# Moving the first output tile's products into the last attention head, and joining two score matmuls of the even stage

## The chip, the cores and the metric

One core of a Trainium2 chip runs the whole program once. The metric is the device time of that core in microseconds (us). TensorE (PE) does matmuls and transposes, with a separate record for each weight load (PEld); VectorE (DVE), ScalarE (ACT) and GpSimd (POOL) do the rest; SyncE (SP) issues most transfers. Each engine works through its own queue in order, and semaphores tie the queues together.

## The reference, cut to what matters

Two layers on 1024 latent and 256 context tokens of width 1024. Layer 0 is an "even" mixer: input projections, a short convolution, an mLSTM over ten chunks of 128 tokens in two directions for four heads of width 256, and an output projection. Layer 1 is latent attention with 16 heads, and again an output projection over 2048 rows, followed by a layer norm:

```
# mlstm, per chunk                       # attention, per head
s   = einsum('bhtd,bhsd->bhts', qc, kc) * w     s = einsum(q_n, k_n) + einsum(q_r, k_r)
num = einsum('bhts,bhsd->bhtd', s, vc) + ...    p = softmax(s * MLA_SCALE)
kw  = kc * w_tok                                o = einsum('bhqk,bkhd->bqhd', p, v)
# after all heads
y_lat = (o_lat * silu(s_lat[3])) @ w_out        # 1024 x 2048 @ 2048 x 1024
h_lat = layer_norm(DEEPNORM_ALPHA * h_lat + g_l * y_lat, ...)
```

## The kernel before, in words

Every float32 product is made of three matmuls on operands split into a high and a low part in the type fp32r: `mm3` (lines 37 to 42) issues high x high, high x low and low x high into one accumulation. ACT makes the high part by a cast, DVE the low part by a subtraction. One weight load goes with each matmul.

**Even stage** (`stage_even`). PE walks through 18 projection tiles a head, and other work is put between them. `prepare(h, c)` (from line 1069) is such work: for a chunk `c` it makes the 128 x 128 scores of keys and queries, two `mm3` (one for each half of the head's width, so six matmuls of 128 columns), and two transposes of the keys, all into one PSUM bank. `prepared(h, c)` (line 913) is DVE's side: it copies the scores to `v_s_all` (line 917) and the turned keys to `v_k_tok` (line 918), and frees the bank. `PREPARED` (line 403) puts the ten chunks two by two at five places of tiles 4 and 5, for four heads. The chunks of such a pair go to two different banks (`e_e` and `e_z` in the rows).

**Attention** (`stage_attend`). A slot is a head `h` and a tile `t` of 128 queries, eight to a head, 128 in all. In a slot PE makes the scores (line 2389: five matmuls for each of 256, 512 and 512 keys) in the three-bank tensor `S`; DVE finds the maximum in two parts and the bias (lines 2281 to 2285); ACT takes the exponential (line 2193); DVE inverts the total (line 2289) and ACT normalises (line 2198). PE's next scores wait for that exponential, since it reads `S` (line 2399). In between PE turns the probabilities of the slot before by ten transposes (`T` operations, line 2376), whose results ACT and DVE split into `t_pt_hi` and `t_pt_lo`. Twice a head PE multiplies them with the values (`PV`, line 2383, 30 matmuls of 512 columns), at `t` = 5 and at `t` = 1 of the next head. In the other slots PE projects queries, keys and values of the next head. The last head, 15, has no next head, so its slots hold no projections. `T`, `PV` and projections write a ring of five PSUM banks in turn, and an operation waits until the one five earlier is read (`RING`, line 2368).

**Output stage** (`stage_out`, layer 1). A token tile's result is 16 steps `k`, each with two halves `o`: six matmuls of 512 columns for one tile and `k`. `first_pair` (line 1479) does tiles 0 and 1 together, `k` by `k`, as weight `k` becomes ready (`w_ok`), with the last three `T` operations before `k` = 1 and the last `PV` before `k` = 2; then tiles 2 to 7 follow one by one. Before it PE waits for the last exponential (`scores_read`) and for the low part of `T(15, 6, 2)` (`ring_read`), whose bank tile 1 takes. Weights are split by ACT (line 1235) and DVE (line 1244): w0, w1 and the first halves of the inputs of tiles 0 and 1 (`m`) in slots 1 and 5 of the last head (`OUT_SPLITS`), w2 to w5 behind the last `T` operations (`OUT_TAIL`), the others in `stage_out` (`REST`). SP loads w8 to w11 after the last scores, w12 after the last `T`, and the second halves of `m` and w13 to w15 after the last `PV`.

Of the kernel before, what the change touches and what calls it, by code (L numbers as in the profile page):

```python
# [6 lines left out]
D = 1024  # L7
CTX, LAT = 256, 1024
T = CTX + LAT
P = 128  # L10
# [5 lines left out]
KM = MIX // P  # L16
# [367 lines left out]
def stage_even(nc, a, keep):  # L384
# [49 lines left out]
    with ExitStack() as ctx:  # L434
# [364 lines left out]
        def _(dve):  # L799
# [239 lines left out]
        def _(pe):  # L1039
# [29 lines left out]
            def prepare(h, c):  # L1069

                t0, bank = c * P, prep_bank(c)
                pe.wait_ge(pj_free_d, dve_free[(h, 3, group_of(c))])
                if c >= 2:
                    pe.wait_ge(prep_ok, prep_at[(h, c - 2)])
                elif h:
                    pe.wait_ge(ht_used, ht_at[(h - 1, 1, 2)])
                else:
                    pe.wait_ge(const_ok, 1)
                    pe.wait_ge(g_kept, 10)
                for j in range(2):  # L1080
                    mm3(nc, bank[:, 0:P], (k_hi[:, j, t0:t0 + P], k_lo[:, j, t0:t0 + P]), (q_hi[:, j, t0:t0 + P], q_lo[:, j, t0:t0 + P]), j == 0, j == 1)
                for j in range(2):
                    last = nc.tensor.transpose(bank[:, (1 + j) * P:(2 + j) * P], k_whole[:, j, t0:t0 + P], ident[:, :])
                last.then_inc(prep_done, 1)

            def state(h, n, d):
# [94 lines left out]
class Output:  # L1181
# [46 lines left out]
    def high(self, act, kind, n, h=None):  # L1228
# [4 lines left out]
        else:  # L1233
            act.wait_ge(self.w_in[n % OUT_HALF], 16 * (n // OUT_HALF + 1))
            self.nc.scalar.copy(self.w_hi[n][:, :], self.w_raw[n][:, :]).then_inc(self.w_hi_ok, 1)

    def low(self, dve, kind, n, h=None):
        if kind == "m":
            b = self.slot(n, h)
            dve.wait_ge(self.m_hi_ok, self.order_of[(n, h)])  # L1240
            self.nc.vector.tensor_tensor(self.m_lo[b][:, :, :], self.m_raw[b][:, :, :], f(self.m_hi[b][:, :, :]), ALU.subtract).then_inc(self.m_ok, 1)
        else:
            dve.wait_ge(self.w_hi_ok, n + 1)
            self.nc.vector.tensor_tensor(self.w_lo[n][:, :], self.w_raw[n][:, :], f(self.w_hi[n][:, :]), ALU.subtract).then_inc(self.w_ok, 1)


def stage_out(nc, a, keep, layer, out=None, block=None, latent=None, tail=None):
# [10 lines left out]
    with ExitStack() as ctx:  # L1258
# [212 lines left out]

        @block.tensor
        def _(pe):
            def products(n, k, o):
                b, i = slot(n, k // H), k % H
                return mm3(nc, y_bank[n % YB][o], (m_hi[b][:, i, :], m_lo[b][:, i, :]), (w_hi[k][:, cols(o)], w_lo[k][:, cols(o)]),
                           k == 0, k == KM - 1)

            def first_pair():

                for k in range(KM):
                    if layer == 1:
                        for op in tail["ring_ops"].get(k, ()):
                            tail["ring_op"](op)
                    pe.wait_ge(w_ok, k + 1)
                    for n in range(2):
                        if k % H == 0:
                            pe.wait_ge(m_ok, order_of[(n, k // H)])
                        for o in range(2):
# [3 lines left out]
                    if k == H - 1:  # L1493
                        last.then_inc(first_half, 1)

            def project(n, between=()):
# [447 lines left out]
def stage_attend(nc, a, keep):  # L1944
# [48 lines left out]
    with ExitStack() as ctx:  # L1993
# [6 lines left out]
        def pair(name, shape, where, step):  # L2000
# [29 lines left out]
        ROW, lq_at, lkv_at = 8 * D, keep["t_at"]["lq"], keep["t_at"]["lkv"]  # L2030
        v_at, prob_at, turn_at = u_at + 16 * T + 24 * LAT, u_at + 32 * T + 24 * LAT, u_at + 40 * T + 24 * LAT
        places = {"w": [lkv_at, lkv_at + 16 * T, lkv_at + 16 * T + ROW, lat_at, lq_at, lq_at + ROW, lq_at + 2 * ROW, lat_at + ROW,
                        u_at + 8 * T, u_at + 16 * T + 8 * LAT, u_at + 16 * T + 16 * LAT, lkv_at + 8 * T, prob_at, v_at, v_at + ROW, w_at],
                  "m": [u_at, u_at + 16 * T, w_at + ROW, pt_at], "res0": pt_at + ROW, "res1": pt_at + ROW + 4 * D, "y0": pt_at + 2 * ROW,
                  "y1": v_at + 2 * ROW, "g_bc": turn_at, "ln_g": w_at + 2 * ROW, "ln_b": w_at + 2 * ROW + 4 * D, "small": turn_at + 4 * LAT}
        last, end = AH - 1, ("PV", AH - 1, 1)
        old, third = ("T", last, QT - 2, 2), [("T", last, QT - 1, g) for g in range(2)]
        y_banks = [[S[:, 0:512], S[:, 512:1024]], [S[:, 1024:1536], ring[at[old] % RING][:, :]], [ring[at[op] % RING][:, :] for op in third]]
# [5 lines left out]
        bank = lambda op: ring[at[op] % RING]  # L2044
        tile = lambda h, t: h * QT + t

        LOADS, load_no = hw.order, hw.load_no
# [13 lines left out]
        def place(op, half):  # L2061
# [6 lines left out]
            if kind == "v":  # L2068
# [5 lines left out]
        tail = {"ring_ops": {1: TAIL[:3], 2: TAIL[3:]}, "scores_read": (exp_ok, tile(last, QT)), "ring_read": (ring_free, at[old]),  # L2074
                "third_banks": (ring_free, at[third[1]]), "values_done": (ring_done, at[end]),
                "queries_split": (qs_ok, AH + 1), "stored": [(og_out[x], 16 * AH) for x in range(2)]}

# [1 line left out]
        def _(sp):  # L2079
# [41 lines left out]
            sp.wait_ge(ring_done, at[("T", last, QT - 1, 2)])  # L2121
            out.load_w(sp, 12)
            store(last, 1)
            sp.wait_ge(ring_done, at[end])
            sp.wait_ge(og_out[0], 16 * AH)
            out.load_m(sp, 0, 1)
            out.load_m(sp, 1, 1)
            for k in range(13, KM):
                out.load_w(sp, k)
            sp.wait_ge(og_out[1], 16 * AH)  # L2130

# [26 lines left out]
        def _(act):  # L2158
# [45 lines left out]
            for h, t in slots:  # L2204
                turned = turned_ops(moved(h, t))
                if not values(h, t):
                    for op in turned[:1]:
                        high(op)
                    exponentials(h, t)
                    for op in turned[1:]:  # L2210
                        high(op)
                    normalise(h, t)
                else:
                    exponentials(h, t)
                    normalise(h, t)
# [12 lines left out]
                if split_here(h, t) and not values(h, t):  # L2228
                    split(*split_here(h, t))
            for op in TAIL:  # L2230
                high(op)
            for piece in OUT_TAIL:
# [3 lines left out]
        def _(dve):  # L2236
# [58 lines left out]
            for h, t in slots:  # L2295
                turned = turned_ops(moved(h, t))
                maximum(h, t)
                earlier = (h, t - 1) if t else (h - 1, QT - 1)
                if split_here(*earlier) and not values(*earlier):
                    hw.low(dve, *split_here(*earlier))  # L2300
# [27 lines left out]
        def _(pe):  # L2328
# [36 lines left out]

            def ring_op(op):
                n, ps = at[op], bank(op)
                if n > RING:
                    pe.wait_ge(ring_free, n - RING)
                if op[0] == "T":  # L2370
                    _, h, t, g = op
                    if g == 0:
# [11 lines left out]
                else:  # L2384
                    weights_ok(op)
                    last = project(op, ps)
                last.then_inc(ring_done, 1)

            def scores(h, t):
                b, tok = h % 2, slice(t * P, (t + 1) * P)  # L2390
# [124 lines left out]
```

## Time and profile before

| | us |
|---|---|
| median of 3 runs (lowest, highest) | 2916.73 (2914.29, 2917.38) |
| the profiled execution's own time | 2915.16 |
| its span, first to last instruction | 2913.4 |
| PE busy | 2861.9 (98%) |
| DVE busy | 1534.6 (53%) |
| ACT busy | 1192.5 (41%) |

A row of the timeline gives the start in us from the span's start, the duration, the engine, line, operation, output and inputs, and in brackets how long the engine was idle before it and what released it. A matmul's duration includes its way through the array, so that the records of neighbouring matmuls overlap; what a matmul costs in a row of matmuls is the distance from its start to the next start.

### The profile page before, as it was taken

Reading aid. Unit: us, or ns where it says so; the run is one execution under the profiler, and the core shown is the slowest. Engines: PE = TensorE matmul, PEld = TensorE weight load, DVE = VectorE, ACT = ScalarE, POOL = GpSimd, SP = SyncE. Lnnn points to the kernel's source line nnn. Section 1 sums busy time; section 2 is a strip of 40 time slices with the busy share of each in tenths; the row PEclk is TensorE's granted clock in tenths of the full one; section 3 lists DMA queues with packets and bytes.
Section 4 is the critical chain, followed back from the end, with each engine's and each line's share of the span. In section 5 each row is a group of like instructions: output and inputs, shape, how many; then the busy total and the mean of one; then the engine's idle time right before and its main releaser. Section 6 shows DMA issues by size and latency. Waiting matters only on the chain. (4 is left out here: it accounts for less than half of the span.)

```text
span 2913.4 us, 38355 instructions
## 1 busy us (share of the span) xinstructions
PE 2861.9 (98%) x15527; PEld 2455.1 (84%) x15527; DVE 1534.6 (53%) x2782; ACT 1192.5 (41%) x1991; POOL 261.1 (9%) x279
## 2 busy tenths in 40 slices
PE   7999999999999999999999999999999999999998
PEld 6888888888888888888887887888888888888787
DVE  6646543655256536554353324665656666666544
ACT  6323312332233223342244214666666666666500
POOL 5100000000000000001320001202102022020000
PEclk9999999999999999999999999999999999999999
DMA  7311131123111311163361320100000101002332
GB/s 210 96 33 46 46 112 31 46 55 112 31 46 46 114 30 46 53 212 102 109 194 42 116 94 26 34 27 30 27 26 27 38 19 34 23 27 98 123 94 79
DMA packets 221505, 200.77 MB, mean 69 GB/s; under 512 B 12085, under 2 KB 193221, under 8 KB 221330
## 3 DMA queue, kind: packets, MB, share of 16 engines
q1 hardware_dynamic: 208578, 184.91, 20.7%
q0 software_dynamic: 2352, 8.17, 0.8%
q10 hardware_dynamic: 10400, 5.24, 0.6%
q8 instruction: 124, 2.03, 0.3%
q14 instruction: 51, 0.42, 0.0%
HBM read 157.34 MB, written 40.95 MB: 68 GB/s over the span
## 5 line engine op out<-in xcount | busy, mean ns | idle before, releaser
L40 PE MATMUL e_pj<-e_u_hi,v_w_hi 128*128 128x512 f32 (+1 forms) x864 | 310.1, 359 | 1.9 <-DVE v_kk_lo L878 1.9
L40 PE MATMUL e_pj<-e_u_hi,e_w_hi 128*128 128x512 f32 (+1 forms) x864 | 308.1, 357 | 1.0 <-PEq L58 1.0
L41 PE MATMUL e_pj<-e_u_lo,v_w_hi 128*128 128x512 f32 (+1 forms) x864 | 308.3, 357 | 0.0
L42 PE MATMUL e_pj<-e_u_hi,v_w_lo 128*128 128x512 f32 (+1 forms) x864 | 308.1, 357 | 0.0
L41 PE MATMUL e_pj<-e_u_lo,e_w_hi 128*128 128x512 f32 (+1 forms) x864 | 306.0, 354 | 0.0
L42 PE MATMUL e_pj<-e_u_hi,e_w_lo 128*128 128x512 f32 (+1 forms) x864 | 305.8, 354 | 0.0
L2177 ACT CAST t_pt_hi<-t_ring 128x512 fp32r<-128x512 f32 (+1 forms) x384 | 181.6, 520 | 233.0 <-PE t_ring L2376 233.0
L2264 DVE TENSOR_TENSOR t_pt_lo<-t_ring,t_pt_hi 128x512 fp32r<-128x512 f32 (+1 forms) x384 | 216.2, 598 | 52.0 <-ACT t_pt_hi L2177 50.7
L2193 ACT ACTIVATE t_prob<-t_scores,t_bias 128x1280 f32<-128x1280 f32 x128 | 170.7, 1334 | 90.9 <-DVE t_bias L2285 90.6
L40 PEld LDWEIGHTS e_pj<-e_u_hi,v_w_hi 128*128 128x128 f32 x864 | 164.9, 191 | 24.5 <-DVE v_kk_lo L878 2.1
L42 PEld LDWEIGHTS e_pj<-e_u_hi,v_w_lo 128*128 128x128 f32 x864 | 164.6, 190 | 23.7
L41 PEld LDWEIGHTS e_pj<-e_u_lo,v_w_hi 128*128 128x128 f32 x864 | 164.8, 191 | 21.4
L42 PEld LDWEIGHTS e_pj<-e_u_hi,e_w_lo 128*128 128x128 f32 x864 | 163.1, 189 | 23.2
L40 PEld LDWEIGHTS e_pj<-e_u_hi,e_w_hi 128*128 128x128 f32 x864 | 163.2, 189 | 22.1 <-issue 1.2
L41 PEld LDWEIGHTS e_pj<-e_u_lo,e_w_hi 128*128 128x128 f32 x864 | 163.3, 189 | 20.6
L2198 ACT ACTIVATE t_prob<-t_prob,t_rec 128x1280 f32<-128x1280 f32 x128 | 177.2, 1384 | 7.4 <-DVE t_rec L2289 7.4
L2376 PEld LDWEIGHTS t_ring<-k_ident,t_prob 128*128 128x128 f32 x1280 | 147.2, 140 | 16.7
L2376 PE MATMUL t_ring<-k_ident,t_prob 128*128 128x128 f32 x1280 | 160.3, 272 | 0.0
L40 PE MATMUL t_scores<-t_kn_hi,t_qn_hi 128*128 128x512 f32 (+1 forms) x384 | 141.5, 369 | 9.0 <-ACT t_prob L2193 7.5
L41 PE MATMUL t_scores<-t_kn_lo,t_qn_hi 128*128 128x512 f32 (+1 forms) x384 | 136.7, 356 | 0.0
L2405 PE MATMUL t_scores<-l_kr_lo,t_qs 128*128 128x512 f32 (+1 forms) x384 | 136.6, 356 | 0.0
L2404 PE MATMUL t_scores<-l_kr_hi,t_qs 128*128 128x512 f32 (+1 forms) x384 | 136.5, 355 | 0.0
(461 smaller groups left out, 6650.7 us busy)
## 6 DMA issues: line engine op xcount, KB each, us to landing
e_w_raw<-in_ev_w_in SPq DMA_DIRECT2D x72, 512.0 KB, 4.7
v_mw<-in_mod_w SPq DMA_DIRECT2D x32, 512.0 KB, 4.0
l_w_raw<-in_od_w_in SPq DMA_DIRECT2D x21, 512.0 KB, 4.0
o_m_raw<-mixT SPq DMA_DIRECT2D x20, 512.0 KB, 5.4
o_w_raw<-in_ev_w_out SPq DMA_DIRECT2D x16, 512.0 KB, 10.4
zgT<-l_lat_q SPq DMA_DIRECT2D x16, 512.0 KB, 3.8
t_zg<-zgT SPq DMA_DIRECT2D x32, 256.0 KB, 2.8
ogT<-t_zg SPq DMA_DIRECT2D x32, 256.0 KB, 2.0
```

The lines of the kernel that those rows point to most:

```text
L40: nc.tensor.matmul(out, whi, xhi, start=first, stop=False)
L41: nc.tensor.matmul(out, whi, xlo, start=False, stop=False)
L42: return nc.tensor.matmul(out, wlo, xhi, start=False, stop=last)
L2177: nc.scalar.copy(dst, src).then_inc(ring_hi, 1)
L2193: nc.scalar.activation(prob[x][:, :], S[:, 0:T], ACT.Exp, bias=bias[x][:, :], accum_out=total[x][:, :]).then_inc(exp_ok, 1)
L2198: nc.scalar.mul(prob[x][:, :], prob[x][:, :], rec[x][:, :]).then_inc(prob_ok, 1)
L2264: nc.vector.tensor_tensor(dst, src, hi, ALU.subtract).then_inc(ring_free, frees(op))
L2376: last = nc.tensor.transpose(ps[:, c * P:(c + 1) * P], prob[t % 2][:, (c0 + c) * P:(c0 + c + 1) * P], ident[:, :])
L2404: nc.tensor.matmul(out, qs[b][:, tok], kr2[0][:, k0:k0 + n], start=False, stop=False)
L2405: last = nc.tensor.matmul(out, qs[b][:, tok], kr2[1][:, k0:k0 + n], start=False, stop=True)
```

## The change: what it does

In the even stage the high and low queries lie in one tensor `q_both`, and one matmul of 256 columns multiplies the high keys with both; a second one, of 128 columns, multiplies the low keys with the high queries. That makes four matmuls for a chunk where there were six. The bank then holds two partial score blocks side by side, and DVE adds them with a `tensor_reduce` over pairs where it copied.

In attention, six steps of output tile 0 (`k` = 0 to 5) are done in slots 2 to 7 of the last head: after the `T` operations, in slot 5 between `PV` and `T`. Weights 0, 2, 3, 4 and 6 are split at the end of slots 0, 2, 3, 4 and 6 (`OUT_ENDS`), on DVE behind the next slot's maximum. Tile 0's banks are two of the ring, so that from `T(15, 1, 0)` on the ring has three banks (`LATE`, `reuse`); the last `PV` goes to the third bank of `S`. Behind the last slot the order is: steps (0,6), (1,0), (1,1), the last `T` operations, (1,2) to (1,4), the last `PV`, (0,7), (1,5) to (1,7), and then both tiles together from `k` = 8. The places of weights and inputs in SBUF change, and with them the order of loads: w8, the second halves of `m` and w9 after the last scores, w10 after the last `T`, w11 to w15 after the last `PV`. The wait `ring_read` is gone.

```diff
-        q_hi, q_lo = s.pair("q", [P, 2, T])
+        q_both = s.sb("q_both", [P, 2, 2, T], F32R)
+        q_hi, q_lo = q_both[:, 0], q_both[:, 1]
...
-                nc.vector.tensor_copy(s_all[:, c, :], bank[:, 0:P])
-                nc.vector.tensor_copy(k_tok[:, :, c, :], bank[:, P:3 * P].rearrange("p (j e) -> p j e", e=P)).then_inc(prep_ok, 1)
+                nc.vector.tensor_reduce(s_all[:, c, :], bank[:, 0:2 * P].rearrange("p (x t) -> p t x", t=P), AX, ALU.add)
+                nc.vector.tensor_copy(k_tok[:, :, c, :], bank[:, 2 * P:4 * P].rearrange("p (j e) -> p j e", e=P)).then_inc(prep_ok, 1)
...
-                    mm3(nc, bank[:, 0:P], (k_hi[:, j, t0:t0 + P], k_lo[:, j, t0:t0 + P]), (q_hi[:, j, t0:t0 + P], q_lo[:, j, t0:t0 + P]), j == 0, j == 1)
+                    nc.tensor.matmul(bank[:, 0:2 * P].rearrange("p (x t) -> p x t", t=P), k_hi[:, j, t0:t0 + P], q_both[:, :, j, t0:t0 + P], start=j == 0, stop=False)
+                    nc.tensor.matmul(bank[:, 0:P], k_lo[:, j, t0:t0 + P], q_hi[:, j, t0:t0 + P], start=False, stop=j == 1)
...
+    def pair_step(self, pe, n, k):
+        pe.wait_ge(self.w_ok, k + 1)
+        if k == 0:
+            pe.wait_ge(self.m_ok, self.order_of[(n, 0)])
+        for o in range(2):
+            last = self.product(n, k, o)
+        return last
...
-            REST = weights(6, 13) + [("m", 0, 1), ("m", 1, 1)] + weights(13, KM)
+            REST = weights(10, KM)
...
-                for k in range(KM):
-                    if layer == 1:
-                        for op in tail["ring_ops"].get(k, ()):
-                            tail["ring_op"](op)
+                for step in tail["steps"] if layer == 1 else ():
+                    last = out.pair_step(pe, *step) if step[0] in (0, 1) else tail["ring_op"](step)
+                if layer == 1:
+                    last.then_inc(first_half, 1)
+                for k in range(H if layer == 1 else 0, KM):
...
-                pe.wait_ge(*tail["ring_read"])
...
+        held, late_from = at[("PV", last - 1, 1)], at[("T", last, 1, 0)]
+        LATE = [(held + 1 + g) % RING for g in range(3)]
+        reuse = lambda op: RING if at[op] < late_from else 3
...
+        y_banks = [[ring[(held + o - 1) % RING][:, :] for o in range(2)], [S[:, 0:512], S[:, 512:1024]], [bank(op) for op in third]]
-        OUT_SPLITS = {(last, 1): [("w", 0), ("m", 0, 0)], (last, 5): [("m", 1, 0), ("w", 1)]}
-        OUT_TAIL = [("w", k) for k in range(2, 6)]
+        OUT_SPLITS = {(last, 1): [("m", 0, 0), ("w", 1)], (last, 5): [("w", 5), ("m", 1, 0)]}
+        OUT_ENDS = {(last, 0): ("w", 0), (last, 2): ("w", 2), (last, 3): ("w", 3), (last, 4): ("w", 4), (last, 6): ("w", 6)}
+        OUT_TAIL = [("w", 7), ("w", 8), ("m", 0, 1), ("m", 1, 1), ("w", 9)]
+        OUT_FILL = {(last, t): (0, t - 2) for t in range(2, QT)}
...
+        tail = {"steps": [(0, 6), (1, 0), (1, 1)] + TAIL[:3] + [(1, 2), (1, 3), (1, 4), end, (0, 7), (1, 5), (1, 6), (1, 7)],
...
             sp.wait_ge(qk_done, tile(last, QT))
-            for k in range(8, 12):
-                out.load_w(sp, k)
+            out.load_w(sp, 8)
+            sp.wait_ge(og_out[0], 16 * AH)
+            out.load_m(sp, 0, 1)
+            out.load_m(sp, 1, 1)
+            out.load_w(sp, 9)
+            sp.wait_ge(ring_done, at[("T", last, QT - 1, 2)])
+            out.load_w(sp, 10)
+            store(last, 1)
+            sp.wait_ge(ring_done, at[end])
+            for k in range(11, KM):
+                out.load_w(sp, k)
...
-                for op in values(h, t) + turned_ops(moved(h, t)) + projections(h, t):
+                for op in values(h, t):
                     ring_op(op)
+                if (h, t) == (AH - 1, 5):
+                    out.pair_step(pe, *OUT_FILL[(h, t)])
+                for op in turned_ops(moved(h, t)) + projections(h, t):
+                    ring_op(op)
+                if (h, t) == (AH - 1, 2):
+                    pe.wait_ge(ring_free, held)
+                if (h, t) in OUT_FILL and t != 5:
+                    out.pair_step(pe, *OUT_FILL[(h, t)])
```

## Rows read from the trace of the kernel before

**Rows 1.** The page: busy time of each engine, share of the span, instructions.
```profile
PE 2861.9 (98%) x15527; PEld 2455.1 (84%) x15527; DVE 1534.6 (53%) x2782; ACT 1192.5 (41%) x1991; POOL 261.1 (9%) x279
```

**Rows 2.** Waits of PE, whole span: us in total, times, longest.
```profile
PE t_scores L40 <- ACT t_prob L2193: 7.5, 5, 2.0
```

**Rows 3.** Timeline of PE, one pair of prepared chunks; columns: start, duration, instruction.
```profile
132.35 0.22 PE L40 MATMUL e_e<-v_q_hi,v_kk_hi 128*128 128x128 f32 x1
...
132.97 0.41 PE L1083 MATMUL e_e<-k_ident,v_k_whole 128*128 128x128 f32 x2
133.13 0.31 PE L40 MATMUL e_z<-v_q_hi,v_kk_hi 128*128 128x128 f32 x1
133.27 0.27 PE L41 MATMUL e_z<-v_q_lo,v_kk_hi 128*128 128x128 f32 x1
...
133.83 0.40 PE L1083 MATMUL e_z<-k_ident,v_k_whole 128*128 128x128 f32 x2
```

**Rows 4.** Timeline of PE, value projections of 256 columns in two segments.
```profile
2607.93 0.28 PE L40 MATMUL t_ring<-l_lkv_hi,t_wk_hi 128*128 128x256 f32 x1
2608.04 0.28 PE L41 MATMUL t_ring<-l_lkv_lo,t_wk_hi 128*128 128x256 f32 x1
```

**Rows 5.** The tile v_s_all (ns min/median/max, first and last start) and DVE's wait for it.
```profile
L917 DVE COPY v_s_all<-e_e x20: 281/292/293, 133.4 to 1074.3; 128x128 f32<-128x128 f32 x20
  PE e_e L1083: 65.5, 15
```

**Rows 6.** Timeline of DVE, slot 3 of head 15: maximum, inverse; then slot 7.
```profile
2687.53 0.96 DVE L2281 TENSOR_REDUCE t_most<-t_scores 128x1 f32<-128x768 f32 x1 [0.58 <-PE t_scores L2405]
2688.66 0.69 DVE L2283 TENSOR_REDUCE t_most<-t_scores 128x1 f32<-128x512 f32 x1 [0.18 <-PE t_scores L2405]
...
2691.04 0.16 DVE L2289 RECIPROCAL t_rec<-t_total 128x1 f32<-128x1 f32 x1 [0.63 <-ACT t_prob L2193]
...
2719.14 1.02 DVE L2264 TENSOR_TENSOR t_pt_lo<-t_ring,t_pt_hi 128x512 fp32r<-128x512 f32 x2 [0.31 <-ACT t_pt_hi L2177]
```

**Rows 7.** Timeline of PE, slots of head 15 and the start of the output stage.
```profile
2678.88 1.25 PE L2376 MATMUL t_ring<-k_ident,t_prob 128*128 128x128 f32 x10
2679.89 0.36 PE L40 MATMUL t_scores<-t_kn_hi,t_qn_hi 128*128 128x256 f32 x1
2680.09 0.28 PE L41 MATMUL t_scores<-t_kn_lo,t_qn_hi 128*128 128x256 f32 x1
...
2688.46 1.25 PE L2376 MATMUL t_ring<-k_ident,t_prob 128*128 128x128 f32 x10
2691.15 0.36 PE L40 MATMUL t_scores<-t_kn_hi,t_qn_hi 128*128 128x256 f32 x1 [1.43 <-ACT t_prob L2193]
...
2716.09 1.25 PE L2376 MATMUL t_ring<-k_ident,t_prob 128*128 128x128 f32 x10
2720.26 0.47 PE L40 MATMUL t_scores<-o_w_hi,o_m_hi 128*128 128x512 f32 x1 [2.92 <-issue]
...
2721.72 0.40 PE L40 MATMUL t_scores<-o_w_hi,o_m_hi 128*128 128x512 f32 x1
...
2723.11 1.25 PE L2376 MATMUL t_ring<-k_ident,t_prob 128*128 128x128 f32 x10
```

**Rows 8.** Timeline of ACT, between the exponentials of slots 3 and 4 of head 15.
```profile
2691.63 1.40 ACT L2198 ACTIVATE t_prob<-t_prob,t_rec 128x1280 f32<-128x1280 f32 x1
2694.75 0.59 ACT L2177 CAST t_pt_hi<-t_ring 128x512 fp32r<-128x512 f32 x1 [1.73 <-PE t_ring L2376]
```

**Rows 9.** The tile o_w_raw: DVE's split of a weight (ns), and loads to landing.
```profile
L1244 DVE TENSOR_TENSOR o_w_lo<-o_w_raw,o_w_hi x32: 1216/1222/1226, 1268.7 to 2749.6; 128x1024 fp32r<-128x1024 f32 x32
DMA to landing us min/median/max: 3.6/7.8/13.4
```

**Rows 10.** Timeline of SP and of ACT: the last loads of weights and their last split.
```profile
2736.33 3.15 SPq L1226 DMA_DIRECT2D o_w_raw<-in_od_w_out  x3
2748.54 1.05 ACT L1235 CAST o_w_hi<-o_w_raw 128x1024 fp32r<-128x1024 f32 x1 [1.19 <-DMA o_w_raw<-in_od_w_out]
```

More of the change, by code:

```diff
@@ L1080, in prepare @@
                 for j in range(2):
-                    mm3(nc, bank[:, 0:P], (k_hi[:, j, t0:t0 + P], k_lo[:, j, t0:t0 + P]), (q_hi[:, j, t0:t0 + P], q_lo[:, j, t0:t0 + P]), j == 0, j == 1)
+                    nc.tensor.matmul(bank[:, 0:2 * P].rearrange("p (x t) -> p x t", t=P), k_hi[:, j, t0:t0 + P], q_both[:, :, j, t0:t0 + P], start=j == 0, stop=False)
+                    nc.tensor.matmul(bank[:, 0:P], k_lo[:, j, t0:t0 + P], q_hi[:, j, t0:t0 + P], start=False, stop=j == 1)
                 for j in range(2):
-                    last = nc.tensor.transpose(bank[:, (1 + j) * P:(2 + j) * P], k_whole[:, j, t0:t0 + P], ident[:, :])
+                    last = nc.tensor.transpose(bank[:, (2 + j) * P:(3 + j) * P], k_whole[:, j, t0:t0 + P], ident[:, :])
                 last.then_inc(prep_done, 1)
@@ L1235, in high, with product @@
             self.nc.scalar.copy(self.w_hi[n][:, :], self.w_raw[n][:, :]).then_inc(self.w_hi_ok, 1)
+    def product(self, n, k, o):
+        b, i, cols = self.slot(n, k // OUT_HALF), k % OUT_HALF, slice(512 * o, 512 * o + 512)
+        return mm3(self.nc, self.y_banks[n % 3][o], (self.m_hi[b][:, i, :], self.m_lo[b][:, i, :]),
+                   (self.w_hi[k][:, cols], self.w_lo[k][:, cols]), k == 0, k == KM - 1)
+    def pair_step(self, pe, n, k):
[5 more added lines that the diff above has]
+        return last
     def low(self, dve, kind, n, h=None):
@@ L1473, in _ @@
         def _(pe):
[L1474 to L1477, printed above, removed]
+            products = out.product
             def first_pair():
-                for k in range(KM):
-                    if layer == 1:
-                        for op in tail["ring_ops"].get(k, ()):
-                            tail["ring_op"](op)
+                for step in tail["steps"] if layer == 1 else ():
[3 more added lines that the diff above has]
+                for k in range(H if layer == 1 else 0, KM):
                     pe.wait_ge(w_ok, k + 1)
@@ L1492, in first_pair @@
                                 last.then_inc(y_half, 1)
-                    if k == H - 1:
+                    if layer == 0 and k == H - 1:
                         last.then_inc(first_half, 1)
@@ L2035, in stage_attend @@
+                  "m": [u_at, u_at + 16 * T, u_at + 16 * T + 16 * LAT, lkv_at + 8 * T], "res0": pt_at + ROW, "res1": pt_at + ROW + 4 * D, "y0": pt_at + 2 * ROW,
                   "y1": v_at + 2 * ROW, "g_bc": turn_at, "ln_g": w_at + 2 * ROW, "ln_b": w_at + 2 * ROW + 4 * D, "small": turn_at + 4 * LAT}
         last, end = AH - 1, ("PV", AH - 1, 1)
-        old, third = ("T", last, QT - 2, 2), [("T", last, QT - 1, g) for g in range(2)]
-        y_banks = [[S[:, 0:512], S[:, 512:1024]], [S[:, 1024:1536], ring[at[old] % RING][:, :]], [ring[at[op] % RING][:, :] for op in third]]
+        held, late_from = at[("PV", last - 1, 1)], at[("T", last, 1, 0)]
@@ new lines, in stage_attend, with bank @@
+        LATE = [(held + 1 + g) % RING for g in range(3)]
+        reuse = lambda op: RING if at[op] < late_from else 3
+        def bank(op):
+            if op == end:
+                return S[:, 1024:1536]
+            return ring[at[op] % RING if at[op] < late_from else LATE[(at[op] - late_from) % 3]][:, :]
+        third = [("T", last, QT - 1, g) for g in range(2)]
+        y_banks = [[ring[(held + o - 1) % RING][:, :] for o in range(2)], [S[:, 0:512], S[:, 512:1024]], [bank(op) for op in third]]
@@ L2042, in stage_attend @@
+        OUT_FILL = {(last, t): (0, t - 2) for t in range(2, QT)}
         block = ctx.enter_context(nc.Block())
-        bank = lambda op: ring[at[op] % RING]
         tile = lambda h, t: h * QT + t
@@ L2072, in place @@
             return pt[half][:, c0:c0 + n, col:col + P], ps[:, 0:n * P].rearrange("p (c e) -> p c e", e=P)
-        tail = {"ring_ops": {1: TAIL[:3], 2: TAIL[3:]}, "scores_read": (exp_ok, tile(last, QT)), "ring_read": (ring_free, at[old]),
+        tail = {"steps": [(0, 6), (1, 0), (1, 1)] + TAIL[:3] + [(1, 2), (1, 3), (1, 4), end, (0, 7), (1, 5), (1, 6), (1, 7)],
+                "scores_read": (exp_ok, tile(last, QT)),
                 "third_banks": (ring_free, at[third[1]]), "values_done": (ring_done, at[end]),
@@ L2118, in _ @@
             sp.wait_ge(qk_done, tile(last, QT))
-            for k in range(8, 12):
-                out.load_w(sp, k)
[L2121 to L2124, printed above, removed]
+            out.load_w(sp, 8)
             sp.wait_ge(og_out[0], 16 * AH)
@@ L2127, in _ @@
             out.load_m(sp, 1, 1)
-            for k in range(13, KM):
+            out.load_w(sp, 9)
[4 more added lines that the diff above has]
+            for k in range(11, KM):
                 out.load_w(sp, k)
@@ L2229, in _ @@
                     split(*split_here(h, t))
+                if (h, t) in OUT_ENDS:
+                    out.high(act, *OUT_ENDS[(h, t)])
             for op in TAIL:
@@ L2297, in _ @@
                 maximum(h, t)
+                if (h, t - 1) in OUT_ENDS:
+                    out.low(dve, *OUT_ENDS[(h, t - 1)])
                 earlier = (h, t - 1) if t else (h - 1, QT - 1)
@@ L2367, in ring_op @@
                 n, ps = at[op], bank(op)
-                if n > RING:
-                    pe.wait_ge(ring_free, n - RING)
+                if op == end:
+                    pe.wait_ge(exp_ok, tile(AH - 1, QT))
+                elif n > RING:
+                    pe.wait_ge(ring_free, n - reuse(op))
                 if op[0] == "T":
@@ L2386, in ring_op @@
                     last = project(op, ps)
-                last.then_inc(ring_done, 1)
+                return last.then_inc(ring_done, 1)
             def scores(h, t):
```

3 lines of the change are left out of this document (1 added, 2 removed).

## The prediction

> **What bounds the kernel now.** The page comes first: PE is busy for 98% of the span, DVE for 53%, ACT for 41% [rows 1]. So time can come only from PE's queue: from fewer or shorter matmuls, or from the little that PE waits. The list of PE's waits comes second. The largest of all is for the exponentials, 7.5 us in five waits [rows 2]. The third view is PE's timeline at the two places of the change. Durations overlap there, so I read distances between starts.
>
> In the even stage a pair of chunks shows the six score matmuls of the first chunk from 132.35 to the transposes at 132.97, 0.62 us, and those of the second from 133.13 to 133.83, 0.70 us [rows 3]. Matmuls of 128 columns follow each other at 0.11 us (the first behind transposes at 0.14, 133.13 to 133.27, the other five at (0.70 - 0.14) / 5 = 0.11). A matmul of 256 columns takes 0.11 us as well, 2607.93 to 2608.04, 0.12 on a mean [rows 4]. Twice the columns cost the same: at 128 columns something that goes with each matmul sets the pace, and that can only be its weight load. Four matmuls should then take about two thirds of the time of six.
>
> In the last head PE stands idle in most slots. Ten transposes take 1.01 us when the next scores start at once (2678.88 to 2679.89). In slot 3 they start at 2688.46 and the next scores at 2691.15: 2.69 - 1.01 = 1.68 us idle. The same distance in slots 2, 4 and 6 gives 1.59, 1.58 and 1.58. At the end of slot 7 it is 2720.26 - 2716.09 - 1.01 = 3.16 us [rows 7]. That one is named "issue" in the row, but ring_read explains it: the low parts of the last T group of slot 6 end at 2719.14 + 1.02 = 2720.16 [rows 6], 0.1 us before PE goes on. From the other slots the exponential alone would have let PE go after about 1.58 us, so 1.58 of the 3.16 is the wait for that bank. Slot 0 has an idle stretch of 2.27 us too, which the change leaves as it is.
>
> **Part 1, joined scores.** First chunk of a pair: the starts would be 0 for the joined matmul, 0.12 for the one of 128 columns, 0.18 and 0.30 for the second half, and the transposes at 0.40. The 0.06 before the third stands because a matmul behind one of 256 columns had its weights loaded early. Saved: 0.62 - 0.40 = 0.22 us. Second chunk: a matmul of 256 columns behind transposes takes 0.20 us to the next (2679.89 to 2680.09 [rows 7]), so 0.20 + 0.11 + 0.12 + 0.11 = 0.54 against 0.70, saved 0.16. A pair saves 0.38 us, and 20 pairs (five places, four heads) save 7.6 us. Bounds: if the joined matmul cost as much as the two it replaces, nothing is saved; if each half took only 0.18, as the first one of a pair might, 40 chunks save (0.66 - 0.36) x 40 = 12 us. I take 7.6, from the rows nearest in form: the value projections also have a moving operand and an output in two segments of 128 [rows 4], and they run at the 256-column pace.
>
> The Trainium skill, page TensorE: Matmul & The Clock Gate, section Back-to-back issue gap, gives for a single stream a distance of N / 2.4 + 2.5 ns, which goes by columns; the same section says that in a stream of load and matmul pairs both set it, and the section on LDWEIGHTS gives 128 / 1.2 = 107 ns a load. By the first rule a chunk has as many columns after as before, and the change would save 2.5 ns for each of 80 matmuls, 0.2 us. By the second it is the estimate 107 x 80 = 8.6 us. The rows, 0.11 us for 128 and for 256 columns, side with the load. The first rule makes a rival below.
>
> DVE's part: 40 copies of 0.292 us [rows 5] become reduces over 256 elements. From 0.96 us for 768 and 0.69 for 512 elements [rows 6] a reduce over 256 is 0.42 us, so DVE has 40 x 0.13 = 5.2 us more. The pairs of a head start at least 4.6 us apart, and DVE stood idle 65.5 us waiting for these very scores [rows 5], so this costs nothing. Bounds: nothing to 0.4 us each (a reduce at the price of 512 elements), and even then the bank is free long before the next pair. Were that cover gone, it would be 5.2 us. PE comes 1.9 us sooner per head to what follows, and nothing there shows PE waiting for an engine that is late by an absolute time.
>
> **Part 2, steps in the last head.** A step is six matmuls of 512 columns: 2721.72 to 2723.11, 1.39 us [rows 7]; with the 0.08 that the first matmul behind transposes costs more, 1.46. It fits into each of the idle stretches of 1.58 to 1.68 in slots 2, 3, 4 and 6, and into the 1.58 of slot 7, with 0.1 to 0.2 left over. The exponential sets the slot's length, so these five steps cost nothing. If they did not fit at all, each would cost its 1.46.
>
> What could lengthen the slot is the splitting put into it. On ACT the high part of a weight is 1.05 us [rows 10] and comes behind the normalising, which ends at 2693.03; ACT is then idle to 2694.75, 1.73 us [rows 8]. It fits. On DVE the low part, 1.22 us, comes behind the maximum, which ends at 2689.35, and the bias, 0.2 us later. The first t_pt_lo of the slot (0.69) follows, and the inverse could start at 2691.45 in place of 2691.04 [rows 6]. The normalising would then start some 0.2 us later, since ACT is busy with t_pt_hi until 2691.63, and the high part of the weight would still end at 2694.3. Behind the inverse wait the two other t_pt_lo, which end 0.1 later, before the next maximum needs DVE. Cost 0, with a bound of 0.4 in five slots, 2 us.
>
> In slot 5 there is no idle stretch to fill, so that step is on the path: 1.46 us. It stands between PV and the transposes, and covers the wait that three banks bring: T(15, 4, 2) takes the bank of PV(15, 0), which DVE reads in 0.7 us, while PE has 1.46 + 0.8 us of other work. The other operations on three banks reuse what was read a slot ago. Each step's weight is split a slot before it, the tightest being w6: its low part ends 1.22 us behind the bias of slot 7, some 0.3 us before step (0,6) may start. Bounds 0 to 0.3.
>
> Behind the last slot: the six steps are gone from there, 6 x 1.39 = 8.3 us. ring_read goes, 1.58 us; what is late next is the exponential, which the step of slot 7 covers. The last T operations need the last normalised probabilities and get them behind three steps (4.2 us), PV starts behind three more, and both find their operands made. Sum of part 2: 8.3 + 1.6 - 1.5 = 8.4 us. Bounds: the idle time there was to fill, 6.4 + 3.2 = 9.6 us, and 8.4 - 2 - 0.3 = 6.1.
>
> SP's queue: w8, two input halves and w9 now go together after the last scores, some 24 us before k = 8 is reached. w10 to w15 and the store of the last head's output come in order. The store waits for DVE to read the last PV, and DVE has w7, w8, two halves and w9 (6.1 us) to split first, but PV itself ends some 18 us behind the last scores, when that should be done. w11 is issued about 1 us behind PV's end. PE then has four steps (5.5 us) and k = 8 to 10 (2.8 each), so it needs w11 13.8 us behind PV and each later one 2.8 after that. Before, the last loads were issued from 2736.33 on and the last was cast at 2748.54, 12.2 us later, with two input halves ahead of them in the queue [rows 10]. Now the first of five needs about 7.8 + 1.05 + 1.22 = 10.1 us by the median landing of 7.8 us [rows 9]. It fits, with 2.7 us to spare, w11 being issued a us behind PV. Cost 0.
>
> **The sum.** 7.6 + 8.4 = 16.0 us. From the profiled execution, 2915.16, that is 2899.2; the median of the runs is 1.6 higher, and I predict against it: 2916.7 - 16.0 = 2900.7 us. About 0.2% (5.8 us) is what can be told from no change here, and the forecast is 0.55%.
>
> **The rivals.** A: matmuls go by columns, and the joined one is as long as two. For it: nothing in the rows shows these operands at 256 columns. Against it: rows 3 and 4. Then only part 2 stays, 2916.7 - 8.4 = 2908.3 us. Chance 0.06; the page's first rule named above says this.
>
> B: the steps in the slots are not hidden, because the splits push back normalising and exponential, and slots 2, 3, 4, 6 and 7 each grow by about 0.8 us. For it: only 0.1 to 0.2 us are to spare in each, and two engines get new work in the loop. Against it: ACT's idle 1.73 us. Part 2 then brings 4.4 us: 2904.7 us. Chance 0.13.
>
> C, slower than before: the last five weights come late. They stand in one row behind a store that stands behind DVE's splits, and if they landed one after the other, at up to 13.4 us each, the last would be ready 5 x 13.4 + 3.3 = 70 us behind PV's end, where PE needs it 25 us behind it: 45 - 16 = 29 us slower, 2946 us. It decides from (25 + 16 - 3.3) / 5 = 7.5 us a weight on. Against it: the last three weights before came 2.2 to 2.5 us apart. Chance 0.02.
>
> D: it does not do what it says: PE is given back its time by a later wait, in the out stage or at a head's end, time within 0.2%, 2914 us. Chance 0.03. The forecast itself, 2897 to 2903.5, has 0.76.
>
> The likeliest gives 2900.7 us. For the range I add the better bounds of both parts (12 + 9.6 = 21.6, so 2895) and B on the other side: 2895 to 2907. Faster 0.94 (forecast, A, B with only a small rest), same 0.04, slower 0.02.
>
> **What would show it.** After the change a pair of chunks takes about 1.27 us where it took 1.65, the joined matmul 0.12 to the next start, 0.20 behind transposes. If its distance is 0.22, A is right. The starts of scores in slots 3, 4 and 5 of the last head keep their distances of 5.6 to 5.7 us, with six matmuls in each and at most 0.3 us idle; distances of 6.4 are B. The first product behind the last slot follows without the 1.6 us for the bank. In the output stage no wait of PE for DVE's o_w_lo at k = 11 to 15; one of more than a us is C. The forecast is wrong if the time is above 2907 or if one part's gain is under half of what stands here.

## The result, and the profile after

The first comparison gave 2894.64 us (median of 4 runs, 2892.95 to 2896.09) against 2915.51 for the kernel before (4 runs), a ratio of 0.9928 with a 95% interval of 0.9915 to 0.9942. I had forecast 2900.7 and a range from 2895: the direction and both mechanisms were right, the gain was larger than forecast by 5 us (20.9 against 16), and the time lies 0.4 us under the range. Ten more runs of the same kernel, in two groups of five that stand with the experiments, gave medians of 2896.39 and 2896.58. Over all 14 its median is 2896.0, and 35 runs of the kernel before have 2915.6 (one more, at 4088.75 us with a granted clock of 0.65, was in the slow state and is left out), so that the gain is 19.6 us.

The page of the changed kernel, which answers to [rows 1]; PE has 80 matmuls fewer:

```profile
span 2893.3 us, 38196 instructions
PE 2851.6 (99%) x15447; PEld 2445.4 (85%) x15447; DVE 1538.2 (53%) x2782; ACT 1190.7 (41%) x1991; POOL 260.9 (9%) x279
```

The waits of PE (in us in total, times, longest). Of the five for the exponential [rows 2] the one of slot 0 is left:

```profile
PE t_scores L40 <- ACT t_prob L2216: 2.0, 1, 2.0
```

A pair of chunks in the changed kernel, from PE's timeline, which answers to [rows 3]. Lines 1082 and 1083 are the joined and the low matmul. The reader is to look at the distances between starts:

```profile
164.42 0.28 PE L1082 MATMUL e_e<-v_q_both,v_kk_hi 128*128 128x256 f32 x1
164.54 0.22 PE L1083 MATMUL e_e<-v_q_both,v_kk_lo 128*128 128x128 f32 x1
164.60 0.34 PE L1082 MATMUL e_e<-v_q_both,v_kk_hi 128*128 128x256 f32 x1
164.77 0.22 PE L1083 MATMUL e_e<-v_q_both,v_kk_lo 128*128 128x128 f32 x1
164.83 0.40 PE L1085 MATMUL e_e<-k_ident,v_k_whole 128*128 128x128 f32 x2
164.98 0.36 PE L1082 MATMUL e_z<-v_q_both,v_kk_hi 128*128 128x256 f32 x1
165.19 0.22 PE L1083 MATMUL e_z<-v_q_both,v_kk_lo 128*128 128x128 f32 x1
165.24 0.34 PE L1082 MATMUL e_z<-v_q_both,v_kk_hi 128*128 128x256 f32 x1
165.42 0.23 PE L1083 MATMUL e_z<-v_q_both,v_kk_lo 128*128 128x128 f32 x1
165.48 0.39 PE L1085 MATMUL e_z<-k_ident,v_k_whole 128*128 128x128 f32 x2
165.63 0.36 PE L40 MATMUL e_pj<-e_u_hi,e_w_hi 128*128 128x256 f32 x1
```

The first chunk takes 0.41 us to its transposes (forecast 0.40, before 0.62), the second 0.50 (forecast 0.54, before 0.70), and each couple of transposes 0.15 in place of 0.16 to 0.17. The whole pair takes 1.21 us in place of 1.65, so 0.44 x 20 = 8.8 us; all twenty pairs of the two traces added up (33.1 and 24.4 us) give 8.7. A low matmul of 128 columns takes 0.05 to 0.06 us to the next start; the joined one behind it takes 0.17, where the first one takes 0.12. The weight loads of the same chunk show an even pace, 0.11 us from start to start (PEld's timeline):

```profile
164.43 0.19 PEld L1083 LDWEIGHTS e_e<-v_q_both,v_kk_lo 128*128 128x128 f32 x1
164.54 0.19 PEld L1082 LDWEIGHTS e_e<-v_q_both,v_kk_hi 128*128 128x128 f32 x1
164.65 0.19 PEld L1083 LDWEIGHTS e_e<-v_q_both,v_kk_lo 128*128 128x128 f32 x1
```

DVE's reduce, from the answer on the tile v_s_all (ns min/median/max; [rows 5] before). It takes 0.42 us, as worked out from the larger reduces, and no engine waits on it:

```profile
L918 DVE TENSOR_REDUCE v_s_all<-e_e x20: 405/425/425, 132.2 to 1064.7; 128x128 f32<-128x256 f32 x20
```

Two slots of the last head from PE's timeline, which answer to [rows 7]: slot 3, from its transposes to the next scores, and slot 7 with what follows it. Each step starts as soon as the transposes are issued:

```profile
2676.77 1.25 PE L2405 MATMUL t_ring<-k_ident,t_prob 128*128 128x128 f32 x10
2677.78 0.48 PE L40 MATMUL t_ring<-o_w_hi,o_m_hi 128*128 128x512 f32 x1
...
2679.46 0.36 PE L40 MATMUL t_scores<-t_kn_hi,t_qn_hi 128*128 128x256 f32 x1
...
2705.76 1.25 PE L2405 MATMUL t_ring<-k_ident,t_prob 128*128 128x128 f32 x10
2706.77 0.48 PE L40 MATMUL t_ring<-o_w_hi,o_m_hi 128*128 128x512 f32 x1
...
2708.35 0.50 PE L40 MATMUL t_ring<-o_w_hi,o_m_hi 128*128 128x512 f32 x1
```

From the transposes to the next scores slot 3 takes 2679.46 - 2676.77 = 2.69 us, exactly as before, but with a step in it. Behind slot 7 the next product comes 2.59 us after the transposes' start, where it came 4.17 us after it. The splits stand where they were expected: in slot 3 DVE makes the low part of weight 2, and at the slot's end, from 2681.20 on, ACT makes the high part of weight 3:

```profile
2677.77 1.22 DVE L1259 TENSOR_TENSOR o_w_lo<-o_w_raw,o_w_hi 128x1024 fp32r<-128x1024 f32 x1
2678.90 0.68 DVE L2289 TENSOR_TENSOR t_pt_lo<-t_ring,t_pt_hi 128x512 fp32r<-128x512 f32 x1
2679.50 0.15 DVE L2314 RECIPROCAL t_rec<-t_total 128x1 f32<-128x1 f32 x1
```
```profile
2681.20 1.06 ACT L1237 CAST o_w_hi<-o_w_raw 128x1024 fp32r<-128x1024 f32 x1
2683.06 0.59 ACT L2200 CAST t_pt_hi<-t_ring 128x512 fp32r<-128x512 f32 x1 [0.80 <-PE t_ring L2405]
```

The inverse comes behind the low part without a stop, and ACT still has 0.80 us to spare. No wait of PE for a weight appears in the output stage.

### The profile page after: what moved, and what is told of

The parts are those of the page before. It is cut to its first block and busy times, and to the rows that moved or that the text cites. A ratio compares the mean times of both kernels' runs of the same rounds, so it can differ in the third digit from the quotient of the medians.

```text
span 2893.3 us, 38196 instructions
## 1 busy us (share of the span) xinstructions
PE 2851.6 (99%) x15447; PEld 2445.4 (85%) x15447; DVE 1538.2 (53%) x2782; ACT 1190.7 (41%) x1991; POOL 260.9 (9%) x279
```

## The experiments

**The change in its two halves**, beside the whole once more. Two accounts of the 19 to 21 us stand against each other in what was expected. Theory S says that the two places bring what their traces show, 8.8 and 8.4 us, and that the rest is scatter. Rival X says that one of the parts brings 3 to 4 us somewhere else as well.

```diff
# joined_only: the kernel before, with the four hunks of the even stage
+        q_both = s.sb("q_both", [P, 2, 2, T], F32R)
...
# tail_only: the changed kernel, with the same hunks undone
+                    mm3(nc, bank[:, 0:P], (k_hi..., k_lo...), (q_hi..., q_lo...), j == 0, j == 1)
```

> The kernel before with the joined score matmuls alone. Theory S: 8.8 us faster than before (0.9970), and every pair of chunks takes 1.21 us from its first matmul to the next projection. My prediction's size: 7.6 us. Rival X, if the hidden rest lies in the even stage: 12 us. Rival A (matmuls go by columns): 0 us.

> The changed kernel with the even stage of before: the last head's steps alone. Theory S and my prediction: 8.4 us faster than before (0.9971), slots 3 to 5 of the last head 5.6 us apart. Rival X, if the rest lies here: 12 us. Rival B (steps not hidden): 4.4 us.

> The changed kernel itself, timed again with the others. Theory S (the parts are worth what their own places show: 8.8 us for the joined scores, 20 pairs at 0.44, and 8.4 us for the last head; the rest of the first comparison is scatter of single executions): 17.2 us faster than before, 0.9941. Rival X (a part brings 3 to 4 us somewhere else as well): 20 to 21 us, 0.9930.

joined_only took 2903.82 us against 2915.5, ratio 0.9958 (0.9946 to 0.9971), 11.7 us faster. tail_only took 2906.11, ratio 0.9968 (0.9956 to 0.9980), 9.4 us faster. The whole took 2896.39, ratio 0.9935 (0.9922 to 0.9947), 19.1 us faster. Rival A is out: the joined scores do bring their time. Rival B too: its 4.4 us lies outside the interval of tail_only (5.8 to 12.8 us). The halves add up to 21.1 us where the whole has 19.1, inside what the intervals leave. Theory S and rival X are not told apart by these times, since both intervals hold 8.8 and 12, or 8.4 and 12.

The traces say more. A pair of chunks takes 1.21 us in joined_only and 1.65 in tail_only. From the start of the first pair to the start of the last one (of 20) lie 940.9 us in the trace of before and 940.8 in tail_only, 934.2 in joined_only and 930.9 to 932.5 in the three traces of the changed kernel. If one takes off what stretches at the lower clock cost behind the modulation sums (below), that is 936.1 us without joined scores and 927.7 to 927.9 with them: 8.3 us, and 19 x 0.434 = 8.2. Between the first pair and the last there is no third place.

**What sets the pace of a chunk's matmuls.**

```diff
# low_wide
-                    nc.tensor.matmul(bank[:, 0:P], k_lo[:, j, t0:t0 + P], q_hi[:, j, t0:t0 + P], start=False, stop=j == 1)
+                    nc.tensor.matmul(bank[:, 0:2 * P].rearrange("p (x t) -> p x t", t=P), k_lo[:, j, t0:t0 + P], q_both[:, :, j, t0:t0 + P], start=False, stop=j == 1)
# no_low: the line is left out
```

> The changed kernel, but the low keys too are multiplied with both halves of the queries: the 80 low matmuls have 256 columns in place of 128, with as many weight loads. If the weight loads set the pace (0.113 us each, four to a chunk), a chunk grows by at most 0.04 us, 0 to 1.5 us in all against the changed kernel. If columns set it once the loads are few, each of the 80 grows by 0.053 us: 4.3 us slower than the changed kernel. In the trace the distance from a low matmul to the next one is 0.06 us now; it should be 0.11 to 0.12, and that from a joined one should fall from 0.17 to 0.12 if loads set the pace.

> The changed kernel without the product of low keys and high queries in the chunk scores (80 matmuls of 128 columns and their loads are left out). What is a low matmul's real price? In the trace the distance from its start to the next is 0.06 us, which would make it 80 x 0.06 = 4.8 us. If its load is the price, at 0.113 us (the load holds up the joined matmul behind it, 0.17 in place of 0.12), it is 80 x 0.113 = 9.0 us; behind transposes some of it may stay, so 7.5 to 9 us faster than the changed kernel. A chunk's two joined matmuls should then be 0.12 us apart.

low_wide took 2895.82 us, ratio to before 0.9930 (0.9918 to 0.9943), not to be told from the changed kernel. The first chunk of a pair in PE's timeline of low_wide, and the start of the second:

```profile
737.02 0.28 PE L1082 MATMUL e_e<-v_q_both,v_kk_hi 128*128 128x256 f32 x1
737.14 0.28 PE L1083 MATMUL e_e<-v_q_both,v_kk_lo 128*128 128x256 f32 x1
737.26 0.28 PE L1082 MATMUL e_e<-v_q_both,v_kk_hi 128*128 128x256 f32 x1
737.38 0.28 PE L1083 MATMUL e_e<-v_q_both,v_kk_lo 128*128 128x256 f32 x1
737.50 0.38 PE L1085 MATMUL e_e<-k_ident,v_k_whole 128*128 128x128 f32 x2
737.63 0.36 PE L1082 MATMUL e_z<-v_q_both,v_kk_hi 128*128 128x256 f32 x1
...
738.33 0.48 PE L40 MATMUL e_pj<-e_u_hi,e_w_hi 128*128 128x512 f32 x1
```

The distances are 0.12 throughout. A wide low matmul takes 0.06 more, and the joined one behind it 0.05 less: the couple of low and joined matmul costs about what it cost, 0.24 us in place of 0.23, and two weight loads at 0.11 us take nearly as long. Only the last low matmul of a chunk, behind which transposes stand, keeps its 0.06. The pair takes 1.31 us, 0.10 more, 2.0 us in all: above the 1.5 that I gave to loads alone and under half of what columns alone would make.

no_low, which leaves the product of low keys and high queries out, took 2887.89 us, ratio 0.9902 (0.9884 to 0.9920), 8.1 us less than the changed kernel's 2896.0. Its pair:

```profile
739.65 0.40 PE L1082 MATMUL e_e<-v_q_both,v_kk_hi 128*128 128x256 f32 x2
739.88 0.38 PE L1084 MATMUL e_e<-k_ident,v_k_whole 128*128 128x128 f32 x2
740.02 0.49 PE L1082 MATMUL e_z<-v_q_both,v_kk_hi 128*128 128x256 f32 x2
740.35 0.38 PE L1084 MATMUL e_z<-k_ident,v_k_whole 128*128 128x128 f32 x2
740.48 0.36 PE L40 MATMUL e_pj<-e_u_hi,v_w_hi 128*128 128x256 f32 x1
```

It takes 0.83 us in place of 1.21, 7.6 us for all 20 and 0.095 for a low matmul, where its distance to the next start is 0.06. The rest shows up at the neighbour, whose distance was 0.17 and not 0.12. So the distance behind a matmul is not its price where widths are mixed.

**The steps in the slots.**

```diff
# no_fill
-        OUT_FILL = {(last, t): (0, t - 2) for t in range(2, QT)}
+        OUT_FILL = {}
...
+        tail = {"steps": [(0, 0), (0, 1), (0, 2), (0, 3), (0, 4), (0, 5), (0, 6),
```

> The changed kernel with steps (0,0) to (0,5) moved out of the slots of the last head to a place ahead of step (0,6); banks, splits and loads stay as they are. My account: five steps were hidden, that of slot 5 was not, so 5 x 1.39 + 0.1 = 7 us slower than the changed kernel, and slots 3 to 5 stay 5.6 us apart. If the splits in the slots cost something that the steps now hide, the slots are longer than 5.7 us. If the steps were not hidden (B), the slots get shorter and the loss is under 4 us. T(15,4,2) waits for DVE's reading of PV without the step of slot 5 ahead of it: up to 0.4 us more.

It took 2903.67 us, ratio to before 0.9953 (0.9937 to 0.9968), 7.7 us more than 2896.0, where 7 was worked out. PE's waits are back as before (the row is of no_fill), and scores still start 5.6 us apart in slots 3 to 5:

```profile
PE t_scores L40 <- ACT t_prob L2216: 7.6, 5, 2.0
```

The end of the span, from slot 0's transposes on, is 7.3 us later than in the changed kernel (last matmul 235.3 us behind them in place of 228.0). So the idle time is really what the steps use, and the splits placed in the slots cost nothing in themselves: with them and without the steps the five waits come to 7.6 us, before to 7.5.

**Two small waits.**

```diff
# step_behind
-                if (h, t) == (AH - 1, 5):
-                    out.pair_step(pe, *OUT_FILL[(h, t)])
...
-                if (h, t) in OUT_FILL and t != 5:
+                if (h, t) in OUT_FILL:
# bank_wait
                 pe.wait_ge(*tail["scores_read"])
+                pe.wait_ge(*tail["ring_read"])      # ring_free, T(15, 6, 2)
```

> The changed kernel with the step of slot 5 behind the transposes in place of ahead of them. If it covers DVE's reading of PV, as I said, PE waits in slot 5 between the first eight transposes and the last two, 0.2 to 0.5 us; if the bank is free anyway, the distance from the first transpose to what follows stays at 1.01 us. In the time this is too small to be told.

> The changed kernel with the wait for the low parts of T(15,6,2) put back ahead of step (0,6). If that wait was the 1.58 us named issue before, the step starts 1.5 us later than in the changed kernel (which has 0.1 us idle there): about 0.1 us behind the end of the two t_pt_lo of slot 7. If the issue was a jump to other code, nothing changes.

PE's timeline of step_behind in slot 5, and of bank_wait behind slot 7:

```profile
2695.28 1.03 PE L2405 MATMUL t_ring<-k_ident,t_prob 128*128 128x128 f32 x8
2696.59 0.44 PE L2405 MATMUL t_ring<-k_ident,t_prob 128*128 128x128 f32 x2 [0.28 <-DVE t_zg L2278]
```
```profile
2710.36 0.47 PE L40 MATMUL t_ring<-o_w_hi,o_m_hi 128*128 128x512 f32 x1 [1.52 <-DVE t_pt_lo L2290]
```

The step in slot 5 does cover a wait, of 0.28 us, for PV's bank. The wait put back costs 1.52 us and now has DVE's name in the row: the two t_pt_lo of that run end at 2710.25, 0.1 us before. The "issue" of 2.92 us in [rows 7] ended at the same distance from the low parts, so it held this wait. In the time both (2896.35 and 2897.09, one run each) can't be told from the changed kernel.

**What is left over: the clock.** The two places are worth 8.8 + 8.4 = 17.2 us by the traces, the times say 19.6. In the windows of the changed kernel (busy time of each engine, then PEclk, DMA share, GB/s) TensorE's granted clock is at half, so 1.2 GHz, from 424 us on:

```profile
422.00:424.00 2.00, 2.00 (x13) 1.75 (x13) 0.00 (x0) 0.00 (x0) 0.00 (x0) 1.00 0.00 0
424.00:426.00 2.00, 2.00 (x6) 1.60 (x5) 0.00 (x0) 0.00 (x0) 0.00 (x0) 0.51 0.00 0
426.00:428.00 2.00, 2.00 (x7) 1.53 (x7) 0.00 (x0) 0.00 (x0) 0.00 (x0) 0.64 0.00 0
```

Matmuls of 512 columns are 0.43 us apart there in place of 0.23. In front of it stand the 32 records of the modulation sums of head 1, two columns each, 3.5 us in one stretch (from 419.05 to the next start at 422.53); another such stretch stands at head 2 (near 722 us). Over the eleven traces of kernels with such stretches the clock fell behind 18 of 22 of them, for 3.4 or 6.8 us. From the first record of the sums to the next pair of chunks PE takes 11.9 us where the clock stays up, 13.5 where it falls for 3.4 us and 15.1 where it falls for 6.8, so that 1.6 or 3.2 us are lost. It differs from execution to execution: 3.2 and 1.6 us in the trace of before, 1.6 and 3.2 in the first of the changed kernel, 3.2 and nothing in the second. I wove the sums into a projection, or cut them in two.

```diff
# woven_sums, and before_woven in the kernel before: in project(), for h in (1, 2), t = 3, j = 2
                 for k in range(KD):
                     last = mm3(...)
+                    for x in range(2 * k, 2 * k + 2) if woven else ():
+                        summed = nc.tensor.matmul(x_bank[:, 2 * x:2 * x + 2], acc[:, x // KD, ...], ones[:, 0:2], start=True, stop=True)
# spread_sums: v = 0 behind project(h, 3, 1), v = 1 behind project(h, 3, 2)
```

> The changed kernel, with the modulation sums of heads 1 and 2 (32 records of two columns in one stretch of 3.6 to 4.1 us) woven into the projection of tile 3, a few behind every three matmuls. Theory S holds that what is left over between the places' 17.2 us and the measured 19 to 21 is the clock: behind these sparse stretches TensorE runs at 1.2 GHz for 3 to 6 us in most executions, 1.5 to 2.7 us lost each, in some executions not at all. Woven in, both stretches should be gone: 2 to 4 us faster than the changed kernel, no stretch at 1.2 GHz near 424 and 722 us. If the clock falls for another reason, nothing changes.

> The same weaving in the kernel before. It should be 3 to 4 us faster than before. The difference between this and woven_sums is the change with two of the chance stretches taken out of both sides: 17.2 us by theory S, 20 or more by rival X.

> The changed kernel with the sums of heads 1 and 2 in two halves of about 2 us, one behind each of two projections, in place of one stretch of 4. If the length of a sparse stretch decides, the clock stays up as with the weaving: 2 to 4 us faster than the changed kernel. If its work in total decides, no gain.

> The changed kernel once more, to stand beside the others on the same chip: 17.2 us faster than before by theory S, 20 to 21 us by rival X.

woven_sums took 2893.24 us, ratio to before 0.9922 (0.9910 to 0.9934); spread_sums 2893.18, ratio 0.9920 (0.9907 to 0.9934); after_third 2896.58, ratio 0.9934 (0.9921 to 0.9946); before_woven 2910.79, ratio 0.9984 (0.9975 to 0.9993). The same windows in woven_sums:

```profile
422.00:424.00 2.00, 2.00 (x15) 1.79 (x14) 0.11 (x1) 0.00 (x0) 0.00 (x0) 1.00 0.03 8
424.00:426.00 2.00, 2.00 (x14) 1.81 (x13) 0.00 (x0) 0.00 (x0) 0.00 (x0) 1.00 0.00 0
426.00:428.00 2.00, 2.00 (x15) 1.75 (x13) 0.00 (x0) 0.00 (x0) 0.00 (x0) 1.00 0.00 0
```

In none of the three traces is a stretch at 1.2 GHz left behind the sums of heads 1 and 2; others stay, at the start and end of the span, near 60 us in one, behind waits of 1.3 to 3.5 us near 115 to 130 and 1755 us, and in spread_sums near 2655 us. The gain is 3.3 us on the changed kernel and 4.8 on the kernel before, where 3 to 4 were expected. With these stretches gone from both sides the change is worth 2910.79 - 2893.24 = 17.6 us, near the 17.2 of its two places. The times alone do not exclude rival X: drawing medians again from the single runs leaves 16.4 to 20.2 us, an estimate. The traces do. They can be cut at the first pair of chunks, the last pair, and the transposes of slot 0 in the last head (us):

| stretch | before | after | before_woven | woven_sums |
|---|---|---|---|---|
| start to first pair | 132.4 | 131.4 | 133.9 | 132.4 |
| first to last pair | 940.9 | 932.5 | 936.2 | 927.8 |
| last pair to slot 0 | 1592.6 | 1590.3 | 1591.4 | 1592.3 |
| slot 0 to the end | 247.6 | 239.2 | 247.5 | 239.2 |

The second and the fourth row hold the two places, and both ways they bring 8.4 and 8.3 to 8.4 us. The first and the third row differ by 1 to 2 us either way, and the third goes by the clock: before and woven_sums have a stretch of 6.8 us at 1.2 GHz near 1755 to 1770 us there, the other two one of 3.4. So no part brings 3 us elsewhere, and rival X falls. Of the 20.0 us between the first two traces, 16.8 are the two places and 3.2 are such differences.

It would also follow that with the stretches there the changed kernel loses less behind its sums (4.8 - 3.3 = 1.5 us). The traces lean the same way, with 4.8 us lost on a mean in the two kernels without joined scores and 3.7 in the nine with them, but these nine run from 1.6 to 6.4, so it is not shown. One stretch works the other way: in six of the eleven traces with the new last head, and in none of the three with the old one, the clock also falls for 3.4 us in slot 0 of that head, behind its wait of 2.0 us. There part 2 is worth 1.6 us less (the last matmul stands 229.5 us behind slot 0's transposes in place of 227.9). Whether that comes with the change or by chance stays open.

woven_sums and spread_sums are each faster than the changed kernel by their medians, but the intervals of the ratios overlap.

## Why the prediction was right and where it failed

**What bounds the kernel** held: all of the gain came out of PE's queue, from fewer matmuls and from its waits.

**Part 1 was right in its mechanism and failed in its size**, at the step "so 0.20 + 0.11 + 0.12 + 0.11 = 0.54 against 0.70". It measured 0.50. I charged the low matmuls of the second chunk the 0.11 us that they had among their like, though I had used 0.06 for one of the first chunk's, behind a joined one. The rows have 0.21, 0.05, 0.18 and 0.06: the low ones are 0.06 and 0.05 shorter, the joined one between them 0.06 longer. In the first chunk the same two errors nearly cancelled (0.12 and 0.10 forecast for its second joined and second low matmul, 0.17 and 0.06 measured), so that its 0.40 against 0.41 was luck. I also left the transposes at 0.16 to 0.17, and they follow at 0.15. The term was 7.6 us and measured 8.8 (8.7 over all twenty pairs). The load's estimate that I gave beside it, 107 ns by the Trainium skill's page TensorE: Matmul & The Clock Gate, section LDWEIGHTS, for 80 loads, 8.6 us, was the better one; the loads stand 0.11 us apart in PEld's rows above. The rule by columns in the section Back-to-back issue gap of the same page of the Trainium skill, rival A, would have made it 0.2 us; joined_only rules it out. DVE's reduce came at the forecast 0.42 us and cost nothing.

**Part 2 held.** Forecast 8.4 us. In the trace of the changed kernel slot 0's transposes start 11.68 us sooner than before (2654.13 against 2665.81) and the span ends 20.0 us sooner, so 8.35 us lie behind that point: 9.7 are gained from slot 7's transposes on (forecast 8.3 + 1.6), and 1.35 are paid ahead of them for the step of slot 5 (forecast 1.46). The slots kept their lengths: scores of slots 3, 4 and 5 start 5.69 and 5.56 us apart (before 5.68 and 5.56). The bank's wait was 1.52 us against 1.58. The step of slot 5 covered 0.28 us. w6 was ready in time (its low part ends at 2707.98, the step starts at 2708.35), and weights 11 to 15 were cast from 2729.78 to 2738.15, ahead of PE all along, against rival C.

**The sum** was then short by 1.2 us from part 1. Of the 6.1 us between 2900.7 and 2894.64 another 1.1 are in my anchor (2916.7 from three runs, where 35 runs have 2915.6), 1.3 in the first four runs of the changed kernel (over 14 they are 2896.0), and 2.4 in what the two places do not hold, of which the medians of the woven kernels (17.6 us) put some 2 on stretches at the lower clock. These the prediction put at nothing without a reason: I had not looked for them. The page of before shows a 9 in every slice of PEclk, and a stretch of 3.4 us does not show in a slice of 73. **The range** failed at the step "12 + 9.6 = 21.6, so 2895". Its lower end came from bounds of the two parts, and the parts stayed well inside them (8.8 and 8.4 us, which from my anchor is 2899.5). Nothing was added for the scatter of a few runs, though the prediction itself gave 5.8 us as what can't be told from no change, nor for a clock that falls in some executions and not in others. The other 4.9 us down to 2894.64 are these. That the miss is only 0.4 us is luck of the first four runs as well: over 14 runs the time, 2896.0, lies inside.

## What to carry to other kernels

In a run of narrow matmuls, count weight loads: here two matmuls that share a stationary operand and have 128 columns each became one of 256 for nearly the price of one (0.12 against 0.11 us). The distance to the next start is no price where widths are mixed: a narrow matmul behind a wide one showed 0.06 us, and leaving it out brought 0.095. Idle time between fixed waits takes in other matmuls for nothing if their operands come a stage early and the split work has its own idle time on each helper engine; a wait named "issue" may be for a second semaphore. Before trusting a difference of 0.1% between single traces, lay out where TensorE's clock was down in each.

## What the runs showed of the hardware

Behind a stretch of 32 matmuls of two columns, 3.5 us at the full clock and without any wait of PE, the granted clock fell to 1.2 GHz in 18 of 22 cases, for 3.4 or 6.8 us, which cost 1.6 or 3.2 us. Cut into two stretches of 1.7 us or woven between wide ones, the same matmuls were followed by no such fall in six cases of three traces.
